# Convolution inside the recurrence before it, and gates as three rounded products, in a two-block kernel

## The chip, the cores and the metric

The kernel runs on one core of one Trainium2 chip. A core has five engines with a queue of instructions each: TensorE (PE in the profile; its weight loads are PEld) multiplies matrices into PSUM, VectorE (DVE) and ScalarE (ACT) work element by element, GpSimd (POOL) too, but it can't reach PSUM, and SyncE (SP) issues the DMAs here. Engines wait for one another through semaphores. The metric is the device time of one execution in microseconds.

## The reference, cut to what matters

Two blocks of two layers each run on a sequence of 512 tokens of width 1024, in float32. The change touches only the first layer of the first block, the even layer:

```
h = rmsnorm(x, norm_pre)
xa, za, xb, gb, gc, zb = split(h @ w_in)                 # 6 x 1024 columns
ua = centred_dwconv(xa, conv_w, left=2) + conv_b         # 4 taps
ya = rg_lru(ua, gates 0, forward) + rg_lru(ua, gates 1, reverse)
ya = ya * silu(za)
yb = gb * centred_dwconv(gc * xb, sc_w, left=1) * silu(zb)   # 3 taps
y = concatenate([ya, yb]) @ w_out
x = x + rmsnorm(y, norm_post)

def rg_lru(u, gate_w, gate_b, lam, reverse):
    r, i = sigmoid(per head of 128: u @ gate_w + gate_b)     # two gates
    log_a = -8 * r * softplus(-lam)
    a = exp(log_a)
    b = sqrt(-expm1(2 * log_a)) * (i * u)
    return scan: h[t] = a[t] * h[t-1] + b[t]
```

There are 8 heads of 128 channels; each has four gate matrices of 128x128 (two gates in each of two directions). The rest, a gated linear attention layer and then a block with feed-forward layers and two kinds of attention, is the same in both kernels.

## The kernel before, in words

Activations lie transposed: 128 channels on the partitions, 512 tokens along the free axis. A large float32 product is made as three products of rounded parts: each operand is split into a high part (rounded to the type fp32r) and a low part (what is left), and the kernel adds high x high, high x low and low x high (`product`, L364 to L366, three matmuls of 128x512 per 128 rows of the sum). GpSimd splits the weights, slot by slot: a slot is 128x1024 weights, a cast (L332) makes the high part and a subtraction (L334) the low one. Raw slots lie in a ring of four, the parts in two buffers each, so GpSimd may split slot s once slot s-2 is used (`slots_used`), and SyncE may load slot s once slot s-4 is split (`w_ready`).

The even layer goes head by head; the code calls a head's 128 channels a channel, numbered 0 to 7, with two copies of its buffers (index `jj`). A channel takes six slots (xa, xb, gc, gb, zb, za), each 24 matmuls into one of four PSUM banks in turn. ScalarE moves each bank to SBUF (`even_moved`, L1325), which frees it for the slot four further on. Below, slot 11 is the last of channel 1, and bank (1,1) is the one of channel 1's second slot.

Per channel the other work is this, in program order. VectorE (`even_dve`): the 4-tap convolution of xa into `ua` (L1778 and three times L1781, signal `ua_ready`), the short 3-tap convolution and its products (L1805 to L1815), then the recurrence: the factors (L1821, L1823, L1825, once per direction), the scans (L1829, L1832) and the sum (L1834, L1836, signal `even_channel_done`). TensorE (`even_gates`, L664): four plain float32 matmuls of the gate weights `gw` with `ua`, behind the six slots of the channel (behind slot 6 for channel 0); the profile shows eight records per channel. ScalarE (`even_act`): the six moves, sigmoids behind the gates (L1337, L1338), exp and tanh (L1346, L1348, signal `decay_ready`), and a square root per direction behind VectorE's factors (L1355). SyncE: for each channel from 2 on, wait for the channel two before to be done, load the gate weights (L594), then the six slots of weights (L591).

Behind channel 7's gates TensorE goes on to the output products (L712 to L714). They need the rounded parts of y: ScalarE makes the high part of each of 16 tiles (L1360), VectorE the low part (L1842), seven tiles of yb first and then seven of ya, behind channel 6. A channel of the profile's timeline is 36.1 us: six slots of 5.44 and the gates.

In the profile's names arena is the region that holds `gw`, `ua`, `xa_pad` and most tiles; ring holds the raw weights and, in the unused end of its slots, a few tiles of the recurrence; w_tails likewise.

## Time and profile before

| | |
|---|---|
| median of 3 runs | 2734.67 us (2733.76 to 2736.94) |
| the profiled execution | 2738.84 us |
| its span in the profile | 2737.1 us |
| TensorE busy | 2702.6 us, 99% |
| VectorE busy | 1324.9 us, 48% |
| GpSimd busy | 1632.3 us, 60% |
| ScalarE busy | 710.4 us, 26% |
| mean granted TensorE clock | 0.999 |

Busy times are of engines that work at the same time, so they don't add up to the span. A matmul record is longer (0.39 us) than its distance to the next (0.23 us), because matmuls are pipelined: TensorE's pace is read from starts. In the timeline a bracket behind a row gives the idle time ahead of it and what ended it.

### The profile page before, as it was taken

The numbers are of one execution on the slowest core, as the hardware profiler recorded it, in microseconds if no ns is written. First come the engines' busy times: TensorE is split into PE (matmuls) and PEld (weight loads), VectorE is DVE, ScalarE is ACT, GpSimd is POOL, SyncE is SP. The second block draws the span as 40 slices with busy tenths as digits, with TensorE's granted clock in tenths as the row PEclk, the third lists the DMA queues.
The fourth block names the chain that finished last, engine by engine and source line by source line (L and its number), as shares of the span: only waits on it lengthen the run. The fifth ranks groups of instructions, "written<-read, shape, count | busy, mean of one in ns | idle before, by whom it ended". The sixth has DMA issues, their size and how long they took to land.

```text
span 2737.1 us, 36086 instructions
## 1 busy us (share of the span) xinstructions
PE 2702.6 (99%) x13190; PEld 2169.5 (79%) x13190; DVE 1324.9 (48%) x1613; ACT 710.4 (26%) x1243; POOL 1632.3 (60%) x949
## 2 busy tenths in 40 slices
PE   9999999999999999999999999999999999999999
PEld 6777778877888888867888888788888776888887
DVE  7888824474532461176440433642244777543242
ACT  4433413343200110184210113410012476211010
POOL 4566755524665666603666666666566789566565
PEclk9999999999999999999999999999999999999999
DMA  4322222202332322201232332333232100233232
GB/s 180 101 92 91 94 93 85 83 26 70 93 116 78 102 96 93 92 9 43 96 107 85 100 100 88 128 100 111 82 98 94 55 2 2 85 100 115 77 97 87
DMA packets 62028, 235.58 MB, mean 86 GB/s; under 512 B 6880, under 2 KB 7008, under 8 KB 61792
## 3 DMA queue, kind: packets, MB, share of 16 engines
q1 hardware_dynamic: 61920, 234.14, 26.6%
q8 instruction: 68, 1.11, 0.2%
q14 instruction: 40, 0.33, 0.0%
HBM read 232.02 MB, written 2.10 MB: 86 GB/s over the span
## 4 chain that ended last, share of the span: by engine, by line
PE 81%; DVE 5%; POOL 4%; PEld 3%; issue 2%; ACT 1%; DVEq 1%; DMA 1%; PEldq 0%; POOLq 0%; ACTq 0%; SPq 0%
PE ps L364 23%; PE ps L365 23%; PE ps L366 23%; POOL arena L2467 4%; PE ps L1045 2%; PE ps L388 1%; PE ps L382 1%; PE ps L383 1%; PE ps L1029 1%; PEld ps L712 1%; PEld ps L713 1%; PEld ps L714 1%; PE ps L1061 1%; DMA ring<-in_even_in 0%; DVE w_tails L1832 0%
## 5 line engine op out<-in xcount | busy, mean ns | idle before, releaser
L334 POOL TENSOR_TENSOR w_lo<-ring,w_hi 128x1024 fp32r<-128x1024 f32 (+2 forms) x382 | 992.3, 2598 | 56.5 <-issue 3.1
L332 POOL CAST w_hi<-ring 128x1024 fp32r<-128x1024 f32 (+2 forms) x382 | 435.9, 1141 | 906.2 <-PE ps L366 720.7
L364 PE MATMUL ps<-hi,w_hi 128*128 128x512 f32 x2064 | 809.9, 392 | 6.1 <-POOL w_lo L334 3.2
L366 PE MATMUL ps<-hi,w_lo 128*128 128x512 f32 x2064 | 804.0, 390 | 0.0
L365 PE MATMUL ps<-lo,w_hi 128*128 128x512 f32 x2064 | 803.8, 389 | 0.0
L364 PEld LDWEIGHTS ps<-hi,w_hi 128*128 128x128 f32 x2064 | 387.8, 188 | 93.6 <-POOL w_lo L334 6.0
L365 PEld LDWEIGHTS ps<-lo,w_hi 128*128 128x128 f32 x2064 | 387.9, 188 | 82.1 <-issue 2.4
L366 PEld LDWEIGHTS ps<-hi,w_lo 128*128 128x128 f32 x2064 | 387.7, 188 | 81.0
L364 PE MATMUL ps<-hid_hi,w_hi 128*128 128x512 f32 x704 | 274.4, 390 | 0.0
L365 PE MATMUL ps<-hid_lo,w_hi 128*128 128x512 f32 x704 | 274.0, 389 | 0.0
L366 PE MATMUL ps<-hid_hi,w_lo 128*128 128x512 f32 x704 | 273.9, 389 | 0.0
L2051 DVE TENSOR_TENSOR hid_lo<-arena,hid_hi 128x512 f32 (+1 forms) x88 | 222.1, 2524 | 80.2 <-ACT hid_hi L1516 80.2
L1514 ACT ACTIVATE ps<-ps 128x512 f32<-128x512 f32 x88 | 51.2, 582 | 629.4 <-DVE ps L2043 629.4
L2067 DVE SCALAR_TENSOR_TENSOR res<-ps,res 128x512 f32<-128x512 f32 x64 | 44.3, 692 | 343.8 <-PE ps L366 343.8
L2048 DVE TENSOR_TENSOR arena<-arena,ps 128x512 f32<-128x512 f32 x88 | 60.5, 688 | 275.4 <-PE ps L366 274.9
L1516 ACT ACTIVATE hid_hi<-arena 128x512 f32 (+1 forms) x88 | 55.7, 633 | 410.8 <-DVE arena L2048 410.8
L364 PEld LDWEIGHTS ps<-hid_hi,w_hi 128*128 128x128 f32 x704 | 132.1, 188 | 28.8 <-POOL w_lo L334 1.3
L366 PEld LDWEIGHTS ps<-hid_hi,w_lo 128*128 128x128 f32 x704 | 132.1, 188 | 27.6
L365 PEld LDWEIGHTS ps<-hid_lo,w_hi 128*128 128x128 f32 x704 | 132.1, 188 | 27.2
L2467 POOL TENSOR_SCALAR arena<-arena 128x512 f32<-128x512 f32 (+3 forms) x124 | 133.2, 1094 | 14.8 <-DVE arena L2343 14.7
L246 DVE SCALAR_TENSOR_TENSOR lo<-res,consts,hi 128x512 fp32r<-128x512 f32 x64 | 117.5, 1845 | 32.0 <-ACT hi L240 31.8
L2043 DVE TENSOR_TENSOR ps<-ps,rinv 128x512 f32<-128x512 f32 x88 | 61.5, 699 | 117.8 <-PE ps L366 107.8
(369 smaller groups left out, 3326.8 us busy)
## 6 DMA issues: line engine op xcount, KB each, us to landing
ring<-in_ffn_in SPq DMA_DIRECT2D x176, 512.0 KB, 3.5
ring<-in_even_in SPq DMA_DIRECT2D x48, 512.0 KB, 4.6
ring<-in_ffn_out SPq DMA_DIRECT2D x32, 768.0 KB, 4.2
ring<-in_ffn_out SPq DMA_DIRECT2D x32, 640.0 KB, 3.8
ring<-in_even_out SPq DMA_DIRECT2D x16, 512.0 KB, 3.5
ring<-in_sb_qk SPq DMA_DIRECT2D x12, 512.0 KB, 3.5
ring<-in_odd_v SPq DMA_DIRECT2D x8, 512.0 KB, 3.5
ring<-in_odd_r SPq DMA_DIRECT2D x8, 512.0 KB, 3.5
```

The source lines that it names most:

```text
L246: nc.vector.scalar_tensor_tensor(lo[:, t, :], res[:, t, :], con("g_" + f)[:, t:t + 1], hi[:, t, :].bitcast(F32), ALU.mult, ALU.subtract).t ...
L332: nc.gpsimd.tensor_copy(high[:, j % 2, 0:cols], ring[:, j, 0:cols])
L334: nc.gpsimd.tensor_tensor(low[:, j % 2, 0:cols], ring[:, j, 0:cols], high[:, j % 2, 0:cols].bitcast(F32), ALU.subtract).then_inc(sem["w_re ...
L364: nc.tensor.matmul(bank, w_hi[:, j % 2, w], x_hi[:, k, :], start=(k == 0), stop=False)
L365: nc.tensor.matmul(bank, w_hi[:, j % 2, w], x_lo[:, k, :], start=False, stop=False)
L366: mm = nc.tensor.matmul(bank, w_lo[:, j % 2, w], x_hi[:, k, :], start=False, stop=(k == kt - 1))
L1045: mm = nc.tensor.matmul(ps[:, bank + e, col:col + T - t2 * P], neg_tri_r[:, :] if t2 == t else neg_ones_r[:, :], part[softplus_of(p, x2)][ ...
L1516: nc.scalar.activation(hid_hi[:, 2 * i + j, :], wide[:, j, :], ACT.Copy)\
L2043: V.tensor_tensor(gate, gate, rinv[:, :], ALU.mult).then_inc(sem["gate_scaled"], 1)
L2048: V.tensor_tensor(wide[:, j, :], wide[:, j, :], up, ALU.mult).then_inc(sem["hidden_wide"], 1)
L2051: V.tensor_tensor(hid_lo[:, 2 * i + j, :], wide[:, j, :], hid_hi[:, 2 * i + j, :].bitcast(F32), ALU.subtract)\
L2467: op = G.tensor_scalar(part, part, coef[:, s % 4, i, e:e + 1], None, ALU.mult)
```

## The change

1. The gates become three products of rounded parts. ScalarE rounds the gate weights of a channel (`gw_hi`, one buffer per `jj`) and its tile (`ua_hi`, one buffer); GpSimd makes the low part of the weights (`gw_lo`) in two halves of 128x256, which it puts between its slots; VectorE makes the low part of the tile (`ua_lo`).
2. VectorE's convolution of channel c+1 moves into the recurrence of channel c, between the factors and the scans, and `ua_lo` of c+1 between the two scans. For this ScalarE moves the first bank of c+1 ahead of the square roots of c; it rounds the tile behind them, ahead of the other five moves.
3. SyncE loads the first four slots of a channel ahead of its gate weights; the wait for a finished channel stands in front of the gate weights and of slots 4 and 5.

```diff
@@ SyncE
                         for jj in range(2):
-                            sp.wait_ge(sem["even_channel_done"], 2 * i + (jj + 3))
-                            gate_weight(i + 1, jj)
                             for n in range(6):
                                 s = 6 * jj + n
+                                if n == RING:
+                                    sp.wait_ge(sem["even_channel_done"], 2 * i + (jj + 3))
+                                    gate_weight(i + 1, jj)
                                 sp.wait_ge(sem["w_ready"], 12 * i + (s + 13))
                                 even_weight(i + 1, s)
@@ TensorE
             def even_gates(i, jj):
-                pe.wait_ge(sem["ua_ready"], 2 * i + (jj + 1))
+                pe.wait_ge(sem["gates_split"], 4 * i + (2 * jj + 2))
                 pe.wait_ge(sem["gates_read"], 2 * i + (jj + 1))
-                pe.wait_ge(gate_landed[jj], 16 * i + 16)
+                pe.wait_ge(sem["ua_low"], 2 * i + (jj + 1))
                 for g in range(4):
-                    mm = nc.tensor.matmul(ps[:, 4 + g, :], gw[:, jj, g * P:(g + 1) * P], ua[:, jj, :],
-                                          start=True, stop=True)
+                    w = slice(g * P, (g + 1) * P)
+                    nc.tensor.matmul(ps[:, 4 + g, :], gw_hi[jj][:, w], ua_hi[:, :], start=True, stop=False)
+                    nc.tensor.matmul(ps[:, 4 + g, :], gw_lo[:, jj, w], ua_hi[:, :], start=False, stop=False)
+                    mm = nc.tensor.matmul(ps[:, 4 + g, :], gw_hi[jj][:, w], ua_lo[:, :], start=False, stop=True)
@@ ScalarE
+            def gates_high_act(i, jj):
+                act.wait_ge(gate_landed[jj], 16 * i + 16)
+                nc.scalar.activation(gw_hi[jj][:, :], gw[:, jj, 0:4 * P], ACT.Copy).then_inc(sem["gates_high"], 1)
+
+            def ua_high_act(i, jj):
+                act.wait_ge(sem["ua_ready"], 2 * i + (jj + 1))
+                nc.scalar.activation(ua_hi[:, :], ua[:, jj, :], ACT.Copy).then_inc(sem["ua_high"], 1)
+
             def even_act(i, jj, c=None):
                 act.wait_ge(sem["even_channel_done"], 2 * i + (jj + 1))
...
+                for n in range(0 if c == 0 else 1, 6):
+                    even_move(i, jj, n, c)
+                    if c == 0 and n == 1:
+                        ua_high_act(0, 0)
...
+                else:
+                    gates_high_act(i + jj, 1 - jj)
                 par = gw[:, jj, 4 * P:4 * P + 16]
                 act.wait_ge(sem["gates_done"], 2 * i + (jj + 1))
+                act.wait_ge(sem["even_channel_done"], 2 * i + (jj + 2))
...
                 a.then_inc(sem["decay_ready"], 1)
+                if c != RG_HEADS - 1:
+                    even_move(i + jj, 1 - jj, 0)
...
                     nc.scalar.activation(rg[d], tg[d], ACT.Sqrt, scale=-1.0).then_inc(sem["root_b_ready"], 1)
+                if c != RG_HEADS - 1:
+                    ua_high_act(i + jj, 1 - jj)
@@ VectorE
+            def convolve(i, jj, c=None):
+                par = gw[:, jj, 4 * P:4 * P + 16]
+                dve.wait_ge(gate_landed[jj], 16 * i + 16)
+                if c != 0:
+                    V.tensor_copy(nsp_c[:, jj, :], nsp2[:, 2 * i + jj, :])
+                dve.wait_ge(sem["even_moved"], 12 * i + (6 * jj + 1 + RING))
+                V.tensor_scalar(ua[:, jj, :], xa_pad[:, jj, 0:T], par[:, 4:5], par[:, 8:9], ALU.mult, ALU.add)
...
+            def ua_lower(i, jj):
+                dve.wait_ge(sem["ua_high"], 2 * i + (jj + 1))
+                V.tensor_tensor(ua_lo[:, :], ua[:, jj, :], ua_hi[:, :].bitcast(F32), ALU.subtract).then_inc(sem["ua_low"], 1)
...
                     V.tensor_tensor(ig[:, d, :], ig[:, d, :], ua[:, jj, :], ALU.mult)
+                if not last:
+                    convolve(i + jj, 1 - jj)
                 for d in range(2):
...
                     V.tensor_tensor_scan(hg[d][:, way], ag[:, d, way], tg[d][:, way], 0.0, ALU.mult, ALU.add)
+                    if d == 0 and not last:
+                        ua_lower(i + jj, 1 - jj)
@@ GpSimd
+            def split_gates(i, jj, half):
+                w = slice(2 * P * half, 2 * P * half + 2 * P)
+                pool.wait_ge(sem["gates_high"], 2 * i + (jj + 1))
+                pool.sem_inc(sem["split_begun"], 1)
+                nc.gpsimd.tensor_tensor(gw_lo[:, jj, w], gw[:, jj, w], gw_hi[jj][:, w].bitcast(F32), ALU.subtract)\
+                    .then_inc(sem["gates_split"], 1)
...
+                for s in range(12):
+                    split_slot(pool, "even_in", 3 * i + (3 + s // RING), s % RING)
+                    if s % 6 in (2, 3):
+                        split_gates(i + 1, s // 6, s % 6 - 2)
```

ScalarE's order behind channel 0, before: tanh, square roots, then the moves of channel 1 (arena<-ps).

```order
L1348 ACTIVATE w_tails<-ring,arena 128x512 x2
L1355 ACT_TABLE_LOAD
L1355 ACTIVATE ring<-w_tails 128x512 [waits factor_ready] x2
L1325 ACTIVATE arena<-ps 128x512 [waits slots_used,even_channel_done]
L1325 ACTIVATE arena<-ps 128x512 [waits slots_used] x3
L1325 ACT_TABLE_LOAD
```

The same place after; gw_hi is rounded between the sixth move and the sigmoids, ua_hi is the rounded tile of channel 1.

```order
L1373 ACTIVATE w_tails<-ring,arena 128x512 x2
L1331 ACTIVATE arena<-ps 128x512 [waits slots_used]
L1382 ACT_TABLE_LOAD
L1382 ACTIVATE ring<-w_tails 128x512 [waits factor_ready] x2
L1339 ACTIVATE ua_hi<-arena 128x512 [waits ua_ready]
L1331 ACTIVATE arena<-ps 128x512 [waits slots_used,even_channel_done]
L1331 ACTIVATE arena<-ps 128x512 [waits slots_used] x2
L1331 ACT_TABLE_LOAD
```

One move went ahead of the square roots; the others now follow a wait for `ua_ready`.

VectorE's order in the recurrence of channel 0, before: factors, scans, sum, then the convolution of channel 1.

```order
L1821 TENSOR_TENSOR w_tails<-arena 128x512
L1823 SCALAR_TENSOR_TENSOR w_tails<-w_tails 128x512
L1825 TENSOR_TENSOR arena<-arena 128x512
L1829 TENSOR_TENSOR w_tails<-arena,ring 128x512 [waits root_b_ready]
L1832 SCALAR_TENSOR_TENSOR w_tails<-arena,w_tails 128x512
L1829 TENSOR_TENSOR w_tails<-arena,ring 128x512 [waits root_b_ready]
L1832 SCALAR_TENSOR_TENSOR w_tails<-arena,w_tails 128x512
L1834 TENSOR_TENSOR w_tails<-w_tails 128x512
L1836 TENSOR_TENSOR arena<-w_tails,arena 128x512
L1773 COPY arena<-arena 128x2 [waits gate_landed_1]
L1778 TENSOR_SCALAR arena<-arena 128x512 [waits even_moved]
```

And after, from the same first instruction on.

```order
L1859 TENSOR_TENSOR w_tails<-arena 128x512
L1861 SCALAR_TENSOR_TENSOR w_tails<-w_tails 128x512
L1863 TENSOR_TENSOR arena<-arena 128x512
L1777 COPY arena<-arena 128x2 [waits gate_landed_1]
L1779 TENSOR_SCALAR arena<-arena 128x512 [waits even_moved]
L1782 SCALAR_TENSOR_TENSOR arena<-arena 128x512 x3
L1869 TENSOR_TENSOR w_tails<-arena,ring 128x512 [waits root_b_ready]
L1872 SCALAR_TENSOR_TENSOR w_tails<-arena,w_tails 128x512
L1788 TENSOR_TENSOR ua_lo<-arena,ua_hi 128x512 [waits ua_high]
L1869 TENSOR_TENSOR w_tails<-arena,ring 128x512 [waits root_b_ready]
L1872 SCALAR_TENSOR_TENSOR w_tails<-arena,w_tails 128x512
```

Five instructions of the convolution and the one of `ua_lo` came into the recurrence.

SyncE's order in the loop, before: the wait for a channel, the gate weights, then the slots.

```order
L594 ISA [waits even_channel_done]
L594 DMA arena<-in_gates 128x528
L619 ISA
L591 ISA [waits w_ready]
L591 DMA ring<-in_even_in 128x1024
```

After, the last of the four slots that are ahead now, the wait, and slot 4.

```order
L597 ISA [waits w_ready]
L597 DMA ring<-in_even_in 128x1024
L624 ISA
L600 ISA [waits even_channel_done]
L600 DMA arena<-in_gates 128x528
L626 REGISTER_ALU
L597 ISA [waits w_ready]
L597 DMA ring<-in_even_in 128x1024
```

The wait for a finished channel went behind four slots of weights.

## Rows read from the trace of the kernel before

**Rows 1.** The page: busy us (share of the span) and instructions.

```profile
PE 2702.6 (99%) x13190; PEld 2169.5 (79%) x13190; DVE 1324.9 (48%) x1613; ACT 710.4 (26%) x1243; POOL 1632.3 (60%) x949
```

**Rows 2.** By stretch: PE, PEld, DVE, ACT, POOL busy us; granted clock, DMA share, GB/s.

```profile
100.00:200.00 100.00, 99.81 (x423) 79.13 (x423) 82.21 (x62) 34.70 (x48) 64.64 (x34) 1.00 0.27 89
...
92.00:95.00 3.00, 3.00 (x9) 2.31 (x8) 0.03 (x1) 2.99 (x5) 2.86 (x2) 0.50 0.54 175
```

**Rows 3.** Timeline, PE and ACT: start us, us, engine, instruction, [idle before <-releaser].

```profile
193.34 0.60 ACT L1325 ACTIVATE arena<-ps 128x512 f32<-128x512 f32 x1 [3.54 <-PE ps L366]
198.78 0.60 ACT L1325 ACTIVATE arena<-ps 128x512 f32<-128x512 f32 x1 [4.84 <-PE ps L366]
...
198.58 3.59 PE L664 MATMUL ps<-arena 128*128 128x512 f32 x8
202.24 0.39 PE L365 MATMUL ps<-lo,w_hi 128*128 128x512 f32 x1
```

**Rows 4.** Timeline of PE: waits, and matmuls behind them.

```profile
13.30 0.65 PE L654 MATMUL ps<-y_lo,w_hi 128*128 128x512 f32 x1 [1.81 <-DVE y_lo L1735]
...
74.20 0.50 PE L364 MATMUL ps<-hi,w_hi 128*128 128x512 f32 x1 [1.28 <-ACT arena L1325]
...
91.53 0.50 PE L364 MATMUL ps<-hi,w_hi 128*128 128x512 f32 x1 [2.71 <-POOL w_lo L334]
...
95.51 0.40 PE L365 MATMUL ps<-lo,w_hi 128*128 128x512 f32 x1
...
165.80 0.50 PE L364 MATMUL ps<-hi,w_hi 128*128 128x512 f32 x1 [0.19 <-POOL w_lo L334]
...
274.73 0.50 PE L364 MATMUL ps<-hi,w_hi 128*128 128x512 f32 x1 [0.33 <-POOL w_lo L334]
...
312.39 0.51 PE L712 MATMUL ps<-lo,w_hi 128*128 128x512 f32 x1 [0.59 <-DVE y_lo L1842]
...
586.29 1.10 PE L849 MATMUL ps<-consts,arena 128*128 128x128 f32 x8 [1.52 <-ACT arena L1473]
```

**Rows 5.** Timeline of SP's queue and POOL; last, the gate weights' time to landing.

```profile
82.19 0.35 SPq L594 DMA_DIRECT2D arena<-in_gates  x1
...
87.53 1.20 POOL L332 CAST w_hi<-ring 128x1024 fp32r<-128x1024 f32 x1 [10.23 <-DMA ring<-in_even_in]
...
DMA to landing us min/median/max: 2.7/2.8/8.3
```

**Rows 6.** Timeline of PE and DVE, gates 0 to the convolution of channel 1.

```profile
52.97 3.59 PE L664 MATMUL ps<-arena 128*128 128x512 f32 x8
...
59.36 0.69 DVE L1805 TENSOR_TENSOR arena<-arena 128x512 f32<-128x512 f32 x1
...
72.92 0.68 DVE L1825 TENSOR_TENSOR arena<-arena 128x512 f32<-128x512 f32 x1
...
81.90 0.16 DVE L1773 COPY arena<-arena 128x2 f32<-128x2 f32 x1
...
82.60 2.41 DVE L1781 SCALAR_TENSOR_TENSOR arena<-arena 128x512 f32<-128x512 f32 x3
```

**Rows 7.** Timeline of POOL and DVE, a factor of channel 4's recurrence.

```profile
209.02 2.66 POOL L334 TENSOR_TENSOR w_lo<-ring,w_hi 128x1024 fp32r<-128x1024 f32 x1
...
209.50 2.72 DVE L1823 SCALAR_TENSOR_TENSOR w_tails<-w_tails 128x512 f32<-128x512 f32 x1
```

**Rows 8.** Timeline of ACT and DVE: first sigmoid, first factor, end of the recurrence.

```profile
199.39 1.28 ACT L1337 ACT_TABLE_LOAD   x1
202.21 0.69 ACT L1337 ACTIVATE ring<-ps,arena 128x512 f32<-128x512 f32 x1 [1.54 <-PE ps L664]
...
208.60 0.82 DVE L1821 TENSOR_TENSOR w_tails<-arena 128x512 f32<-128x512 f32 x1 [5.33 <-ACT w_tails L1348]
...
228.65 0.16 DVE L1773 COPY arena<-arena 128x2 f32 x1
```

**Rows 9.** Timeline of PE and DVE at the end of the layer.

```profile
307.51 3.59 PE L664 MATMUL ps<-arena 128*128 128x512 f32 x8
...
308.86 6.49 DVE L1842 TENSOR_TENSOR y_lo<-arena,lo 128x512 fp32r<-128x512 f32 x7 [1.57 <-ACT lo L1360]
```

**Rows 10.** Groups of POOL's instructions by shape: busy us, mean ns.

```profile
L2461 POOL TENSOR_TENSOR arena<-arena 128x248 f32<-128x248 f32 x8 | 4.8, 604 | 0.0
```

## What I predict, and how it follows

> **What bounds the kernel now.** I read the page first: TensorE is busy 2702.6 us, 99% of the span [rows 1], so only TensorE's own work and its few waits can move the time. The change touches the even layer alone, the first 310 us, so I went on to the busy times by stretch: in its steady part VectorE is busy 82 of 100 us [rows 2]. The reader should see there that the engine that feeds TensorE has little to spare. Next come TensorE's gate products in the timeline [rows 3] and every idle stretch before a matmul of this layer [rows 4]. There are two kinds: a wait for ScalarE to empty a bank (74.20) and waits for GpSimd's split weights (91.53, 165.80, 274.73). The rows of the DMA queue say where the second kind comes from: in the loop the queue waits for a whole channel to be done, issues the gate weights at 82.19 and only then the next projection slots, so GpSimd idles 10.23 us for them [rows 5].
>
> **The gate products.** A channel's four gates begin at 198.58 and the second matmul behind them at 202.24. A slot of 24 matmuls takes 5.44 us (two bank moves stand 5.44 apart), 0.227 each, so four gates cost 202.24 - 198.58 - 0.23 = 3.43 us [rows 3]. Twelve matmuls of rounded parts, of the same 128x512 shape, cost 12 x 0.227 = 2.72. Saved: 8 x 0.71 = **5.7 us**, all on TensorE's path. The bound above is nothing saved, if the new operands ran at another pace; the existing products of rounded parts say they don't.
>
> **The waits that go.** The projection DMAs of a channel's first four slots no longer wait for a channel to be done. So the waits at 91.53 (2.71), 165.80 (0.19) and 274.73 (0.33) go. The first also cost clock: the ten matmuls from 91.53 to 95.51 took 3.98 us where 2.27 is their pace, so 1.7 more: from 92 to 95 the granted clock is 0.50 [rows 2], the 1.2 GHz level. The same slow start shows behind the 1.81 wait at 13.30, and the 1.52 at 586.29 is the longest that I found without it [rows 4]. The wait at 74.20 (1.28) goes too, since the move of the next channel's first bank now stands ahead of the square roots. With 0.1 of slow start behind each: 4.4 + 0.3 + 0.4 + 1.4 = **6.5 us**.
>
> **The new wait in channel 1.** The moves of banks 1 to 5 of the next channel now stand behind the rounding of its convolved tile, and this behind the convolution, which stands behind VectorE's six factor instructions. TensorE needs bank (1,1) empty to begin slot 11. Gates 0 begin at 52.97 [rows 6], end at 55.69, and four slots later it is 77.45. VectorE: the low part of the first tile (0.7) puts the chain behind it 0.7 later, so the short convolution begins at 60.1 and not 59.36. From there to the end of the sixth factor instruction before took 73.60 - 59.36 = 14.2 us, so 74.3. The convolution with its first instructions is 3.1 us (81.90 to 85.01, [rows 6]). If only its last instruction meets GpSimd, the tile is ready at 78.0; adding 0.60 for the rounding and 0.60 for the move, as a bank move's row, bank 1 is free at 79.2, a wait of 1.8. The other end: VectorE instructions with two operands in SBUF wait for a running GpSimd instruction (started 0.48 behind a subtraction of 2.66, a factor took 2.72 and ended 0.54 behind it, [rows 7], where a free one of its kind takes about 0.7, as 72.92 in [rows 6]). TensorE runs 0.7 ahead of before here, so GpSimd's subtraction of slot 11 starts at 73.9, before the last factor instruction; that one ends at 76.9, and two of the three long convolution instructions stand behind the cast and the subtraction of slot 12 (77.7 to 81.6). The tile is ready at 82.4, the bank free at 83.6: a wait of 6.2. I take 6.2, since the 0.7 shifts work that way on both engines. With 1.7 of clock behind it: **+7.9** (bounds +1.8 and +7.9).
>
> Before, the convolution of channel 1 ran unhindered (three instructions in 2.41 at 82.60, [rows 6]), in the gap in which GpSimd idled until 87.53 for its DMA [rows 5]. Now the gap is closed and the convolution stands among the splits.
>
> The Trainium skill ("SBUF — State Buffer", section "Who interferes with whom") says that the two engines share a port pair as an exclusive lock, and that the one that issues second is blocked until the first has ended. The rows agree (ended 0.54 behind the other's end). It speaks against the place to which the convolution moves; if the two engines only shared bandwidth there, this term would be near its lower end and the total some 6 us lower.
>
> **The two added splits per channel on GpSimd.** A 128x248 GpSimd subtraction takes 0.60 [rows 10], so about 0.65 each. They stand behind slots 2 and 3, where GpSimd idles: cast and subtraction take about 3.9 of a slot's 5.44 us (the subtraction 2.66, [rows 7], the cast 1.2, [rows 5]). Nothing on the path; without that cover 0.65 each, at most 1.3 a channel. The queue's wait for a channel to be done now holds up the weights of slots 4 and 5 only; they land some 5 us behind it and are wanted 20 us later, so nothing.
>
> In ScalarE's order of the two kernels the reader sees the rounding of the tile come between the square roots and the moves, in VectorE's the convolution between the factors and the scans, and in the queue's the wait go behind four weights.
>
> **The loop of the recurrence.** The gate weights of channel c+2 are now fetched behind channel c, and ScalarE rounds them before the sigmoids of c+1. Done(c) to landing is 0.2 + 2.8 [rows 5], rounding 0.6, table load 1.3, sigmoids to the first factor 208.60 - 202.21 = 6.4 [rows 8]: 11.3. The recurrence took 228.65 - 208.60 = 20.05, and now holds the convolution (3.1) and the low part (0.7) as well: 35.1 with no more lock waits, 36.8 with one of 1.7 more. TensorE's period becomes 6 x 5.44 + 2.72 = 35.37. Where the loop is longer, VectorE falls behind by up to 1.4 a channel, and the slack at bank 1 (about 4 us in the steady state) is gone after three. I put **+1.0** on it, one such wait (bounds 0 and +6.8, five of them).
>
> **The output products.** They need the low parts of y, the first of them behind channel 6. Before, the first stood at 308.86, 1.35 behind the start of gates 7 (307.51), and TensorE waited 0.59 for the third [rows 4, 9]. After, gates 6 begin at 77.45 + 6.2 + 5.44 + 1.7 (gates 1) and 5 x 35.37 later, 267.6. Channel 5 is done about there, the recurrence of 6 starts 11.3 to 12 later and takes 20.05 + 3.8, and up to 2 more of lock: channel 6 is done between 303 and 305.8. The first low part is 0.7 more if free, 2.7 if it meets GpSimd: 304 to 308.5. TensorE wants it 38.1 behind gates 6, at 305.7. I take 2.5 us of wait, since locks have decided every such place so far; it is over the 1.81 that cost clock: 2.5 + 1.7 - 0.7 = **+3.5** (bounds 0 and +3.8).
>
> **Sum**: -5.7 - 6.5 + 7.9 + 1.0 + 3.5 = +0.2 us. The profiled execution took 2738.84, so 2739.0; against the median of the three runs, 2734.67, this is 2734.9.
>
> **Rivals.**
> 1. *The convolution slips through (faster).* The wait at slot 11 is at its lower end, under the 1.81 that cost clock: -5.7 - 6.5 + 1.8 + 0 + 3.5 = -6.9, with the end wait at its lower bound -10.4. For it: the lock waits are a matter of tenths. Against it: VectorE is shifted late and GpSimd early. About 2726. Chance 0.22.
> 2. *The loop is longer than TensorE's period (slower).* With 36.8 against 35.37 TensorE waits 1.4 for bank 1 in each of channels 3 to 7: -5.7 - 6.5 + 7.9 + 6.8 + 3.5 = +6.0, so 2740.7. It decides from a loop of about 36.2. For it: VectorE's 82%, and the closed gap. Against: a lock wait may fall on idle time. Chance 0.15.
> 3. *The clock does not fall in the new waits*: -3.4, 2731.5. It is inside the range of the forecast. Chance 0.10.
> My forecast, gain and new waits cancelling: 0.53.
>
> **Range and chances.** 0.2% is 5.5 us, about what a measurement of this kernel tells from no change. Faster by more: rival 1, 0.22. Slower by more: rival 2, 0.15. Within: 0.63. The range, 2726 to 2741, holds the forecast and most of both; the forecast's own is 2731 to 2738.
>
> **What would show it.** Right: twelve matmuls at 0.227 per channel in 2.7 us; no TensorE wait on the split weights behind gates 1; one wait of 2 to 6 us before slot 11 for ScalarE's move, some 21.8 us behind gates 0, and slow matmuls behind it; VectorE instructions of 2.7 us in the convolution; a wait of about 2.5 us on VectorE at the first output product. Wrong: no wait at slot 11 (then 2726 or less), or one in most channels (2740).

## The result, and the profile after

The changed kernel takes 2745.53 us (median of 7 runs, 2744.01 to 2746.0), the kernel before 2734.67 (7 runs, 2733.76 to 2738.95). The ratio is 1.0032 with a 95% interval of 1.0023 to 1.0042: slower by 0.3%. I had forecast 2734.9 and a range up to 2741; the time lies outside.

The two profiled executions stand 6.8 us apart (2738.84 and 2745.67), the medians 10.9. The one of before lay high among its own runs, which scatter from 2733.7 to 2739.3 in all that follows (their median was 2736.2 to 2736.8 in samples of 21 to 33). The traces place the loss that they hold: the first matmul of line 382, the next layer's, starts at 408.67 us before and 415.07 after, 6.4 later, and what follows it takes 2328.4 and 2328.8. So I compare kernels by that start as well. It names the place; the medians say how much. Where in the kernel before its runs differ is open, since only one of them was traced.

The page of after, first part (busy us, share of the span, instructions), answers to [rows 1]:

```profile
PE 2697.5 (98%) x13222; PEld 2175.6 (79%) x13222; DVE 1315.6 (48%) x1621; ACT 718.6 (26%) x1259; POOL 1647.8 (60%) x965
```

TensorE is busy 5.1 us less than before, and the kernel is slower. So the time went into waits. The waits of PE up to 420 us say into which (total us, times, longest):

```profile
PE ps L364 <- ACT arena L1331: 13.7, 6, 7.1
PE ps L721 <- DVE y_lo L1884: 2.7, 1, 2.7
```

Six waits for ScalarE to empty a bank, and one for the low part of y. The timeline of PE shows them one by one, and the gates of a channel between two of them; it answers to [rows 3, 4]:

```profile
84.99 0.79 PE L364 MATMUL ps<-hi,w_hi 128*128 128x512 f32 x1 [7.14 <-ACT arena L1331]
...
88.57 0.41 PE L366 MATMUL ps<-hi,w_lo 128*128 128x512 f32 x1
...
158.40 0.49 PE L364 MATMUL ps<-hi,w_hi 128*128 128x512 f32 x1 [0.66 <-ACT arena L1331]
...
195.59 0.49 PE L364 MATMUL ps<-hi,w_hi 128*128 128x512 f32 x1 [1.47 <-ACT arena L1331]
...
201.16 0.39 PE L672 MATMUL ps<-ua_hi,gw_hi 128*128 128x512 f32 x1
...
203.88 0.39 PE L364 MATMUL ps<-hi,w_hi 128*128 128x512 f32 x1
...
232.71 0.49 PE L364 MATMUL ps<-hi,w_hi 128*128 128x512 f32 x1 [1.47 <-ACT arena L1331]
269.88 0.49 PE L364 MATMUL ps<-hi,w_hi 128*128 128x512 f32 x1 [1.46 <-ACT arena L1331]
307.09 0.49 PE L364 MATMUL ps<-hi,w_hi 128*128 128x512 f32 x1 [1.55 <-ACT arena L1331]
318.29 0.47 PE L721 MATMUL ps<-lo,w_hi 128*128 128x512 f32 x1 [2.70 <-DVE y_lo L1884]
```

The twelve products of rounded parts take 203.88 - 201.16 = 2.72 us. The wait at slot 11 is 7.14, and the first eight matmuls behind it take 3.58 where eight take 1.82, so 1.76 more, the usual 0.1 of slow start included. Then there is a wait in each of the channels 3 to 7, and 232.71 - 195.59 = 37.12 is the period, where TensorE's own work is 35.37.

The slot-11 wait, read from VectorE, GpSimd and ScalarE (timeline of each):

```profile
74.64 2.88 DVE L1863 TENSOR_TENSOR arena<-arena 128x512 f32<-128x512 f32 x1
77.45 0.69 DVE L1777 COPY arena<-arena 128x2 f32<-128x2 f32 x1
78.05 1.32 DVE L1779 TENSOR_SCALAR arena<-arena 128x512 f32<-128x512 f32 x1
79.46 4.33 DVE L1782 SCALAR_TENSOR_TENSOR arena<-arena 128x512 f32<-128x512 f32 x3
```

```profile
74.31 2.65 POOL L334 TENSOR_TENSOR w_lo<-ring,w_hi 128x1024 fp32r<-128x1024 f32 x1
76.94 1.18 POOL L2446 TENSOR_TENSOR gw_lo<-arena,gw_hi 128x256 fp32r<-128x256 f32 x1
78.06 1.04 POOL L332 CAST w_hi<-ring 128x1024 fp32r<-128x1024 f32 x1
79.24 2.34 POOL L334 TENSOR_TENSOR w_lo<-ring,w_hi 128x1024 fp32r<-128x1024 f32 x1
```

```profile
83.82 0.63 ACT L1339 ACTIVATE ua_hi<-arena 128x512 fp32r<-128x512 f32 x1 [8.44 <-DVE arena L1782]
```

The last factor instruction and the convolution stand among four GpSimd instructions that follow each other almost without a gap (0.14 us at most), and take 9.2 us where such instructions took 3.8 before (0.68 and 3.1, [rows 6]). The copy ends at 78.14, 0.02 behind the gate split that ran beside it. Such time, in which a VectorE instruction is held up by a running GpSimd instruction, is called a lock wait below; the profile counts it as busy time of VectorE. The tile is ready at 83.8 and the bank free at 85.

The loop of a steady channel (DMA queue, ScalarE, VectorE):

```profile
206.35 0.33 SPq L600 DMA_DIRECT2D arena<-in_gates  x1
```

```profile
209.13 0.64 ACT L1335 ACTIVATE gw_hi<-arena 128x512 fp32r<-128x512 f32 x1 [7.17 <-DMA arena<-in_gates]
```

```profile
203.51 2.63 DVE L1878 TENSOR_TENSOR arena<-w_tails,arena 128x512 f32 x1 [0.17 <-issue]
...
217.46 1.77 DVE L1859 TENSOR_TENSOR w_tails<-arena 128x512 f32<-128x512 f32 x1 [6.21 <-ACT w_tails L1373]
...
226.44 4.99 DVE L1782 SCALAR_TENSOR_TENSOR arena<-arena 128x512 f32<-128x512 f32 x3
...
240.63 2.63 DVE L1878 TENSOR_TENSOR arena<-w_tails,arena 128x512 f32 x1 [0.17 <-issue]
```

A channel is done at 206.14 (203.51 + 2.63). Then the gate weights are fetched, ScalarE has waited 7.17 us for them, rounds them, loads its table, does the sigmoids and the exp and tanh, and the first factor starts at 217.46: 11.3 us. The recurrence ends at 243.26, 25.8 later. 11.3 + 25.8 = 37.1, TensorE's new period. The ring closes on itself: done, gate weights, rounding, sigmoids, recurrence, done.

### The profile page after: what moved, and what is told of

Same layout as the page of the kernel before. It is cut to its first block, busy times and chain, and to the rows that moved or that the text cites. A ratio compares the mean times of both kernels' runs of the same rounds, so it can differ in the third digit from the quotient of the medians.

```text
span 2743.9 us, 36206 instructions
## 1 busy us (share of the span) xinstructions
PE 2697.5 (98%) x13222; PEld 2175.6 (79%) x13222; DVE 1315.6 (48%) x1621; ACT 718.6 (26%) x1259; POOL 1647.8 (60%) x965
## 4 chain that ended last, share of the span: by engine, by line
PE 76%; DVE 8%; POOL 4%; PEld 3%; DVEq 2%; ACT 2%; issue 2%; DMA 1%; PEldq 0%; ACTq 0%; POOLq 0%; SPq 0%
PE ps L364 21%; PE ps L366 21%; PE ps L365 21%; POOL arena L2522 4%; PE ps L1054 2%; PE ps L388 1%; PE ps L382 1%; PE ps L383 1%; DVE arena L1782 1%; PE ps L1038 1%; PEld ps L721 1%; PEld ps L722 1%; PEld ps L723 1%; DVE w_tails L1861 1%; DVEq L1867 1%
## 5 line engine op out<-in xcount | busy, mean ns | idle before, releaser
L364 PE MATMUL ps<-hi,w_hi 128*128 128x512 f32 x2064 | 808.7, 392 | 16.0 <-ACT arena L1331 13.7
L365 PE MATMUL ps<-lo,w_hi 128*128 128x512 f32 x2064 | 803.9, 389 | 0.0
L364 PEld LDWEIGHTS ps<-hi,w_hi 128*128 128x128 f32 x2064 | 387.8, 188 | 101.9 <-issue 10.5
L365 PEld LDWEIGHTS ps<-lo,w_hi 128*128 128x128 f32 x2064 | 387.9, 188 | 81.5 <-issue 1.4
L364 PE MATMUL ps<-hid_hi,w_hi 128*128 128x512 f32 x704 | 274.4, 390 | 0.0
L365 PE MATMUL ps<-hid_lo,w_hi 128*128 128x512 f32 x704 | 273.9, 389 | 0.0
L364 PEld LDWEIGHTS ps<-hid_hi,w_hi 128*128 128x128 f32 x704 | 132.1, 188 | 28.8 <-POOL w_lo L334 1.3
L365 PEld LDWEIGHTS ps<-hid_lo,w_hi 128*128 128x128 f32 x704 | 132.1, 188 | 27.4
L246 DVE SCALAR_TENSOR_TENSOR lo<-res,consts,hi 128x512 fp32r<-128x512 f32 x64 | 100.9, 1585 | 31.9 <-ACT hi L240 31.7
```

What stands on the lines that cost most here:

```text
L246: nc.vector.scalar_tensor_tensor(lo[:, t, :], res[:, t, :], con("g_" + f)[:, t:t + 1], hi[:, t, :].bitcast(F32), ALU.mult, ALU.subtract).t ...
L364: nc.tensor.matmul(bank, w_hi[:, j % 2, w], x_hi[:, k, :], start=(k == 0), stop=False)
L365: nc.tensor.matmul(bank, w_hi[:, j % 2, w], x_lo[:, k, :], start=False, stop=False)
```

## Experiments

Theory T: two causes. The slot-11 wait comes from VectorE's chain (factors, convolution) meeting GpSimd's splits; the waits of the later channels come from the loop "channel done, gate weights fetched and rounded, sigmoids, recurrence", which at 37.1 is longer than TensorE's 35.4. Rivals stand with each experiment. Each kernel was timed beside the kernel before on one chip; the experiments used two chips, so kernels are compared by their ratios to it, given with 95% intervals. The last column is the time from the layer's first matmul of line 364 (at about 25 us) to the first of line 382. The start alone also holds what happened ahead of the change's work: 24.75 us before, 24.99 in the changed kernel, 23.34 with late rounding and early decay terms together, 26.10 with bank 1 first.

| kernel | median us (range, runs) | ratio | start of L382 | L364 to L382 |
|---|---|---|---|---|
| before | 2734.67 (2733.76 to 2738.95, 7) | | 408.67 | 383.92 |
| changed | 2745.53 (2744.01 to 2746.0, 7) | 1.0032 (1.0023 to 1.0042) | 415.07 | 390.08 |
| new queue order alone | 2740.96 (2738.46 to 2742.35, 11) | 1.0013 (1.0004 to 1.0022) | 411.05 | 386.17 |
| rounded gates alone | 2740.99 (2740.4 to 2744.98, 11) | 1.0019 (1.001 to 1.0028) | 412.92 | 388.06 |
| convolution and queue, plain gates | 2731.44 (2729.82 to 2731.84, 11) | 0.9981 (0.9972 to 0.999) | 401.77 | 376.93 |
| the same, decay terms early | 2732.16 (2730.4 to 2732.58, 11) | 0.9985 (0.9976 to 0.9994) | 402.63 | 377.60 |
| changed, old queue | 2757.75 (2756.39 to 2759.35, 5) | 1.0079 (1.0066 to 1.0093) | 427.3 | 402.30 |
| changed, late rounding | 2739.41 (2737.76 to 2740.54, 11) | 1.001 (1.0001 to 1.0019) | 410.09 | 384.61 |
| changed, bank 1 first | 2743.66 (2740.41 to 2746.54, 11) | 1.0025 (1.0016 to 1.0035) | 412.78 | 386.68 |
| changed, decay early | 2741.8 (2740.12 to 2743.02, 11) | 1.0018 (1.0009 to 1.0027) | 412.01 | 387.03 |
| changed, late rounding, decay early | 2733.59 (2731.57 to 2734.57, 11) | 0.9989 (0.998 to 0.9998) | 402.19 | 378.85 |
| changed, all three moves | 2734.9 (2733.48 to 2737.43, 11) | 0.9996 (0.9987 to 1.0005) | 404.25 | 379.27 |
| changed, short subtraction | 2726.74 (2725.31 to 2727.11, 5) | 0.9963 (0.9949 to 0.9977) | 396.94 | 371.70 (L365 to L383 there) |

**Gate weights rounded behind tanh.** ScalarE no longer waits for their DMA ahead of the sigmoids.

```diff
-                else:
-                    gates_high_act(i + jj, 1 - jj)
...
                 if c != RG_HEADS - 1:
                     even_move(i + jj, 1 - jj, 0)
+                    gates_high_act(i + jj, 1 - jj)
```

> The changed kernel, with ScalarE's rounding of the next channel's gate weights moved from ahead of the sigmoids to behind the tanh. Theory (the loop): in the changed kernel ScalarE waits 7.17 us for the gate weights' DMA ahead of each steady channel's sigmoids, which makes the loop from one finished channel to the next 37.1 us against TensorE's 35.4. With the rounding out of the loop the five waits of 0.66 to 1.55 us for bank 1 go and 6.6 us with them; the 7.1 us wait at slot 11 stays, a wait of 2 to 3 at the first output product too: about 2739. Rival (VectorE alone is too slow, through its lock waits with GpSimd): the waits stay, 2745.

2739.41, and the traces differ by 5.0 up to line 382 (5.5 from 25 us on). PE's waits, then VectorE's first factor and the end of its recurrence:

```profile
85.47 0.79 PE L364 MATMUL ps<-hi,w_hi 128*128 128x512 f32 x1 [7.13 <-ACT arena L1331]
230.11 0.49 PE L364 MATMUL ps<-hi,w_hi 128*128 128x512 f32 x1 [0.40 <-ACT arena L1331]
```

```profile
211.35 1.50 DVE L1858 TENSOR_TENSOR w_tails<-arena 128x512 f32<-128x512 f32 x1 [1.31 <-ACT w_tails L1371]
...
238.04 2.64 DVE L1877 TENSOR_TENSOR arena<-w_tails,arena 128x512 f32 x1 [0.17 <-issue]
```

The 6.6 us of the later channels fell to 0.8 (0.40 at 230.11 and again at 302.02) and the slot-11 wait stayed: two causes, and the second is the loop. But the loop got less short than the edit says. The channel before was done at 204.94, so the first factor follows 6.4 us behind it instead of 11.3, 4.9 less; the recurrence takes 240.68 - 211.35 = 29.3 instead of 25.8, 3.5 more, since it now meets more of GpSimd's splits. The period is 35.7, just above TensorE's 35.37.

**Bank 1 of the next channel moved ahead of the rounding of its tile.**

```diff
-                for n in range(0 if c == 0 else 1, 6):
+                for n in range(0 if c == 0 else 2, 6):
...
                 if c != RG_HEADS - 1:
+                    even_move(i + jj, 1 - jj, 1)
                     ua_high_act(i + jj, 1 - jj)
```

> The changed kernel, with the move of the next channel's second bank ahead of the rounding of its tile. Theory (VectorE's chain sets the pace, ScalarE's order only says where TensorE notices it): the waits at slot 5 of each channel go, but TensorE then waits for the low part of the tile ahead of gates 1 (some 5 us), later channels eat up the slack, and the output products wait more; in all 1 to 5 us less than the changed kernel, 2741 to 2744. Rival (ScalarE's order alone is the cause): all 13.7 us of waits and 1.6 of slow clock go, 2731.

2743.66, in the expected range. The wait for the bank became one for the low part of the tile, one slot later. PE, then VectorE:

```profile
90.41 0.77 PE L672 MATMUL ps<-ua_hi,gw_hi 128*128 128x512 f32 x1 [6.00 <-DVE ua_lo L1789]
```

```profile
80.58 4.38 DVE L1783 SCALAR_TENSOR_TENSOR arena<-arena 128x512 f32<-128x512 f32 x3
...
89.60 0.66 DVE L1789 TENSOR_TENSOR ua_lo<-arena,ua_hi 128x512 fp32r<-128x512 f32 x1
```

ScalarE's order alone is not the cause. TensorE wants the gates at 90.41 - 6.00 = 84.41. The tile is ready at 84.96, only 0.55 later, and rounded 0.7 behind that; its low part ends at 90.26, because a product (1.35) and a scan (3.21, where a free one takes 1.23) stand ahead of it in VectorE's order. So most of this wait is the place of the low part. A kernel with the low part right behind the rounding was not run.

**Decay terms ahead of the reciprocal of the norm** (17 small VectorE instructions, 6.8 us in the changed kernel, that stood ahead of channel 0's short convolution).

```diff
-            rinv_dve(dve, "even_pre")
             nsp2 = nsp.rearrange("p (c d) -> p c d", d=2)
+            dve.drain()
+            decay_terms((11, 9, 7, 5, 3, 1))
...
+            V.tensor_copy(nsp_c[:, 0, :], nsp2[:, 0, :]).then_inc(sem["nsp_ready"], 1)
+            rinv_dve(dve, "even_pre")
...
                     scale_plain(5)
-                    decay_terms((11, 9, 7, 5, 3, 1))
```

> The changed kernel, with VectorE's small decay terms moved from channel 0 into its idle 7 us ahead of the first rinv. Theory: VectorE's chain in channel 0 begins 6 to 7 us earlier, so the wait at slot 11 shrinks from 7.1 to about 1 and its slow clock (1.6) goes; the loop of 37.1 per channel stays, with waits of 1.5 at slot 5: about 7 us less, 2738. Rival (the slot-11 wait is made of lock waits that come back wherever the chain starts): under 2 us less, 2744.

2741.8, between the 2738 of the theory and the 2744 of the rival: half of what I had expected. PE's timeline:

```profile
80.50 0.50 PE L364 MATMUL ps<-hi,w_hi 128*128 128x512 f32 x1 [2.02 <-ACT arena L1331]
117.69 0.49 PE L364 MATMUL ps<-hi,w_hi 128*128 128x512 f32 x1 [1.48 <-ACT arena L1331]
...
314.70 0.77 PE L721 MATMUL ps<-lo,w_hi 128*128 128x512 f32 x1 [2.70 <-DVE y_lo L1885]
```

The slot-11 wait fell from 7.14 to 2.02 with no slow clock behind it, but the waits of the loop begin at channel 2 instead of 3 and are 1.48 from the start. In the changed kernel the long wait had given VectorE a lead that the loop then used up. So the two causes share one account: what the first gives back, the second takes, as long as the loop is longer than TensorE's period.

**The new queue order alone, in the kernel before.**

```diff
-                            sp.wait_ge(sem["even_channel_done"], 2 * i + (jj + 3))
-                            gate_weight(i + 1, jj)
                             for n in range(6):
                                 s = 6 * jj + n
+                                if n == RING:
+                                    sp.wait_ge(sem["even_channel_done"], 2 * i + (jj + 3))
+                                    gate_weight(i + 1, jj)
```

> The kernel before, with only the new order of SyncE's queue (four slots of weights ahead of the wait for a finished channel). Theory: the waits for split weights at 91.53 (2.71 and 1.7 of clock), 165.80 and 274.73 go, but GpSimd then splits where it idled, so the convolution of channel 1 runs into locks and gates 1 wait for it: between -4 and +2 us against before, 2731 to 2737. Rival (the queue part is a plain gain): -5.1, 2729.6.

2740.96: this edit only lets DMAs go earlier and makes the kernel slower by 4 us. Both my theory's range (2731 to 2737) and the rival's gain of 5 missed; what I had named, locks in the convolution and gates waiting for it, is there, but larger. PE, VectorE, and PE's window from 90 to 92 us (us, busy and instructions, granted clock, DMA share, GB/s):

```profile
90.20 6.61 PE L665 MATMUL ps<-arena 128*128 128x512 f32 x8 [4.86 <-DVE arena L1782]
96.25 0.80 PE L364 MATMUL ps<-hi,w_hi 128*128 128x512 f32 x1
```

```profile
85.21 4.94 DVE L1782 SCALAR_TENSOR_TENSOR arena<-arena 128x512 f32<-128x512 f32 x3
```

```profile
90.00:92.00 2.00, 1.80 (x2) 0.50 0.53 121
```

The 2.71 us wait for weights is gone, and GpSimd is no longer idle. The convolution of channel 1, which had run in 2.41 in that gap [rows 6], now takes 4.94, and the gates wait 4.86 for it and then run at 1.2 GHz. They take 96.25 - 90.20 - 0.23 = 5.8 us instead of 3.43. Waits and clock together: 1.14 + 4.86 + 2.4 = 8.4, against 6.2 before (1.28 + 2.71 + 1.7 + 0.19 + 0.33), 2.2 more; the traces say 2.3 from 25 us on.

**Rounded gates alone**, convolution and queue as before (`ua_hi` is rounded behind the fifth move).

```diff
-                for n in range(0 if c == 0 else 1, 6):
+                for n in range(6):
                     even_move(i, jj, n, c)
-                    if c == 0 and n == 1:
-                        ua_high_act(0, 0)
+                    if n == (1 if c == 0 else 4):
+                        ua_high_act(i, jj)
...
+                else:
+                    convolve(i, jj, c)
+                    ua_lower(i, jj)
```

> The kernel before with only the gates as three products of rounded parts; convolution and queue as before, ScalarE rounds the tile behind its fifth move, VectorE makes the low part right behind the convolution. Theory: 0.71 us per channel are gained on TensorE, but the queue's wait for a finished channel already has GpSimd just in time (0.19 and 0.33 us late), so TensorE waits for split weights by about what it gained and by the 0.7 us of the low part: 2735 to 2741. Rival (the products are a gain of their own): 2731.

2740.99. PE's timeline:

```profile
77.96 0.80 PE L364 MATMUL ps<-hi,w_hi 128*128 128x512 f32 x1 [5.69 <-ACT arena L1330]
...
204.39 0.50 PE L364 MATMUL ps<-hi,w_hi 128*128 128x512 f32 x1 [0.92 <-POOL w_lo L334]
241.05 0.51 PE L364 MATMUL ps<-hi,w_hi 128*128 128x512 f32 x1 [0.95 <-POOL w_lo L334]
```

The wait at 77.96 comes from the locks too: the move stands behind the square roots, and the last factor that they need ended at 76.8. The 5.7 us that TensorE saves are paid back in the other channels as well: 36.66 from wait to wait, where before it was 36.1. The recurrence takes 21.3 us there, and 20.1 before, and the queue had no room for it (waits of 0.19 and 0.33 before).

**Convolution and queue, with plain float32 gates.**

```diff
                 for g in range(4):
-                    w = slice(g * P, (g + 1) * P)
-                    nc.tensor.matmul(ps[:, 4 + g, :], gw_hi[jj][:, w], ua_hi[:, :], start=True, stop=False)
-                    nc.tensor.matmul(ps[:, 4 + g, :], gw_lo[:, jj, w], ua_hi[:, :], start=False, stop=False)
-                    mm = nc.tensor.matmul(ps[:, 4 + g, :], gw_hi[jj][:, w], ua_lo[:, :], start=False, stop=True)
+                    mm = nc.tensor.matmul(ps[:, 4 + g, :], gw[:, jj, g * P:(g + 1) * P], ua[:, jj, :],
+                                          start=True, stop=True)
```

(the roundings and splits of gate weights and tile are taken out with it)

> The changed kernel with the gates as plain float32 products again, so without the roundings on ScalarE, the low part of the tile on VectorE and the gate splits on GpSimd: the moved convolution and the queue's new order alone. Theory: ScalarE's moves no longer stand behind the convolution and the gate weights' landing is off ScalarE's path, so the waits for bank 1 go; gates 1 wait about 1 to 3 us for the convolved tile; 2731 to 2736. Rival (the convolution inside the recurrence costs time by itself, since it delays the scans): steady waits of over 1 us per channel stay, 2743 or more.

2731.44: faster than both kernels, by 0.19% against before. From 25 to 330 us PE has two waits left; the expected one of gates 1 isn't there. One is this, the other (0.78) is for split weights at 316.73, as before:

```profile
305.46 0.50 PE L719 MATMUL ps<-lo,w_hi 128*128 128x512 f32 x1 [0.72 <-DVE y_lo L1872]
```

So two parts of the change are worth having together, and the third, which saves 5.7 us on the engine that is 99% busy, turns the gain into a loss. In the loop, its rounding ahead of the sigmoids and its low part in the recurrence lengthen the ring, while it shortens TensorE's period to below it: with plain gates a first factor follows a finished channel by 6.4 us where TensorE is not waited for (channels 1 to 2), and the recurrence takes 25.0, so the ring could go round in 31.4, and TensorE's period is 36.1. At slot 11, no bank move stands behind a rounded tile any more. The convolution in the recurrence alone, with plain gates and the old queue, was not run.

**Late rounding and early decay terms together.**

> The changed kernel with both edits that helped alone: gate weights rounded behind the tanh, and VectorE's decay terms ahead of rinv. Theory: the wait at slot 11 is 2 us (as with the early decay terms alone), the steady waits go (as with the late rounding alone), a wait of 2 to 3 at the first output product stays: 5.0 + 3.1 us under the changed kernel plus up to 2 more, since the early start is no longer lost in the loop: 2734 to 2737. Rival (the two gains are the same one): 2739.

2733.59, a little under the expected 2734 to 2737 and 11.9 less than the changed kernel. The traces say 12.9 less up to line 382, but 1.65 of it lies ahead of 25 us, where this execution lost no clock behind a wait of 1.82 at 13.48 us. From 25 us on it is 11.2, and alone the two moves gave 5.5 and 3.1: once the loop is short the early terms give 5.8. The slot-11 wait is 1.46; the output wait:

```profile
304.70 0.47 PE L721 MATMUL ps<-lo,w_hi 128*128 128x512 f32 x1 [2.77 <-DVE y_lo L1884]
```

**All three moves.**

> The changed kernel with all three moves: rounding of the gate weights behind tanh, bank 1 of the next channel ahead of the rounding of its tile, decay terms early. Without the bank's move it took 2733.59, with waits of 1.46 (slot 11), 0.89, 0.40 and 0.40 for banks and 2.77 at the output. Theory: the wait for bank 1 goes, a wait for the low part of the tile ahead of the gates comes in its place and is some 1.1 shorter (as in the kernel with the bank's move alone); the 2.77 at the output stays. 2731 to 2733. Rival (the move of the bank only delays the tile, and the sum stays): 2733.5 to 2735.

2734.9: the rival's figure. The bank waits went, but 0.83 and 1.17 for split weights and a longer output wait (3.49) came; the clock is 0.66 from 306 to 311 us, as it is in the kernel with two moves. Moving one more thing forward no longer helped; from 25 us on the two traces differ by only 0.4.

**Plain gates with early decay terms.**

> The kernel with plain float32 gates, the convolution in the recurrence and the new queue order took 2731.44 us. Here the decay terms move ahead of the reciprocal of the norm as well. Theory (the end of VectorE's recurrence decides only where TensorE waits for it): the kernel with plain gates has no wait for a bank in the whole layer, only 0.5 to 0.8 at places that don't depend on the decay terms, so this gives at most 1 us: 2730.5 to 2731.5. Rival (the decay terms are themselves on the path to the first slots): the 2 to 4 us that the same edit gave to the kernels with rounded gates come again: 2727.5 to 2729.5.

2732.16, and a start of line 382 of 402.63 against 401.77: no gain, and if anything a little slower. Where TensorE had no wait but the 0.7 at the output that VectorE decides, an earlier VectorE was worth nothing. This also speaks against the rival that the decay terms are a cost of their own.

**The changed kernel with the old queue order.**

> The changed kernel with the old order of the queue: the wait for a finished channel stands ahead of all six slots. Theory (the new queue order is what makes room for the longer recurrence): before, TensorE's wait for the split weights of a channel's first slot was 0.2 to 0.3, so nothing was left; the recurrence now holds the convolution and the low part (3.8 us and locks) and ends later, and each of channels 2 to 7 waits 3 to 5 us for split weights: 2755 to 2770. Rival (the queue's order is worth only its waits in the kernel before, and GpSimd's idle time takes the locks away from the convolution, as it did before): 2740 to 2750.

2757.75, as the theory said. PE, VectorE (channel 1's convolution) and GpSimd behind it:

```profile
82.30 0.79 PE L364 MATMUL ps<-hi,w_hi 128*128 128x512 f32 x1 [4.43 <-ACT arena L1330]
95.98 0.51 PE L364 MATMUL ps<-hi,w_hi 128*128 128x512 f32 x1 [2.79 <-POOL w_lo L334]
...
291.35 0.80 PE L364 MATMUL ps<-hi,w_hi 128*128 128x512 f32 x1 [5.33 <-POOL w_lo L334]
```

```profile
78.68 2.42 DVE L1781 SCALAR_TENSOR_TENSOR arena<-arena 128x512 f32<-128x512 f32 x3
```

```profile
92.16 1.28 POOL L332 CAST w_hi<-ring 128x1024 fp32r<-128x1024 f32 x1 [14.04 <-DMA ring<-in_even_in]
```

Here the rival was right in one thing: with GpSimd idle the convolution ran free (2.42 instead of 4.33) and the slot-11 wait is 2.7 shorter. But then five of the six channels 2 to 7 wait for their weights (2.79, 2.33, 2.29, 4.02 and 5.33). The new queue order harms alone and is worth 12 us together with the convolution in the recurrence and the rounded gates: an idle stretch of one engine was the free time of another.

**GpSimd's subtraction cut short.**

```diff
-            nc.gpsimd.tensor_tensor(low[:, j % 2, 0:cols], ring[:, j, 0:cols], high[:, j % 2, 0:cols].bitcast(F32),
+            n_low = 128 if name == "even_in" and not (isinstance(i, int) and i == 0) else cols
+            nc.gpsimd.tensor_tensor(low[:, j % 2, 0:n_low], ring[:, j, 0:n_low], high[:, j % 2, 0:n_low].bitcast(F32),
```

> The changed kernel, with GpSimd's subtraction cut to the first 128 of 1024 columns for the even layer's input slots behind the first four (the low parts of the other columns are old values; its numbers are not the reference's). It takes away most of the time that GpSimd keeps VectorE out and nothing else. Theory (lock waits): VectorE's 2.7 us instructions shrink to about 0.7 in the even layer, the waits at slot 11, in the steady channels and at the first output product all go: some 17 to 20 us under the changed kernel, 2727. Rival (the new order of instructions alone is too long): the waits stay within 2 us in sum, 2743.

2726.74, 0.3 from the expected 2727. No wait at slot 11, none in the loop; at the first output product 1.27 us stay, which I had expected to go. VectorE's timeline of a steady channel:

```profile
200.24 0.73 DVE L1860 TENSOR_TENSOR w_tails<-arena 128x512 f32<-128x512 f32 x1 [7.85 <-ACT w_tails L1374]
...
206.54 2.41 DVE L1783 SCALAR_TENSOR_TENSOR arena<-arena 128x512 f32<-128x512 f32 x3
...
216.23 0.69 DVE L1879 TENSOR_TENSOR arena<-w_tails,arena 128x512 f32 x1 [0.17 <-issue]
...
235.65 0.74 DVE L1860 TENSOR_TENSOR w_tails<-arena 128x512 f32<-128x512 f32 x1 [7.91 <-ACT w_tails L1374]
```

The recurrence takes 216.92 - 200.24 = 16.7 us, and in the changed kernel 25.8: 9 us of every steady channel come from VectorE's lock waits behind GpSimd's long subtractions. The two gate splits per channel are still in this kernel, and without the long subtractions they make no wait on TensorE. The period is 35.41, TensorE's own. This agrees with the Trainium skill ("SBUF — State Buffer", section "Who interferes with whom"): the engine that issues second is blocked until the first has ended; the four rows from 74.64 on show that a two-element copy (0.69, where it took 0.16 before, [rows 6]) is blocked too; it ends with GpSimd's instruction, within 0.02.

## Why the prediction was wrong, point by point

| term | predicted | measured in the traces |
|---|---|---|
| gates | -5.7 | -5.7 (2.72 per channel) |
| waits that go | -6.5 | -6.5, all four gone |
| slot 11 | +7.9 | +8.9 (7.14, 1.76 of clock and slow start) |
| loop of the recurrence | +1.0 | +7.1 (0.66 + 1.47 + 1.47 + 1.46 + 1.55, and 0.1 of slow start each) |
| output products | +3.5 | +2.1 (2.70 - 0.59, no clock lost) |
| sum | +0.2 | +5.9 (the starts of line 382: +6.4; 0.24 of it is there already at 25 us, ahead of the change's work) |

- **The step that failed is the loop term**, "I put +1.0 on it, one such wait (bounds 0 and +6.8, five of them)". The mechanism was named, its parts were near (11.3 from done to the first factor, as measured), and its upper end is what came. I took the recurrence as 20.05 + 3.8 and treated a further lock wait as a chance. It took 25.8, 1.95 more. With the short subtraction it took 16.7, so some 9 of the 25.8 are lock waits behind the long subtractions; less the 3.8 that moved in, 16.7 leaves 12.9, so the old 20.05 held some 7 (an estimate from these figures), and 2 came on top. I had counted such a further lock wait once, in one channel. The recurrences of channels 3 to 6 take 25.8, 25.8, 26.0 and 25.8: the same meetings came back in every channel, so one more wait counted once per channel. Why they repeat was not tested; GpSimd's splits follow TensorE, and in this loop TensorE follows VectorE. The experiment with late rounding took 5.8 of the 6.6 us away: 4.9 less from done to the first factor, of which the recurrence took 3.5 back in lock waits.
- **Slot 11**: the choice of 6.2 between 1.8 and 6.2 was right, for the reason given, and was 0.9 too small: the two-element copy and the first convolution instruction were blocked as well. The copy was held by the gate split at 76.94, a GpSimd instruction that the prediction put at nothing on the path, and the split at 218.63 (1.19) held a factor of the steady recurrence 0.4 longer. No kernel without only these splits was run.
- **Waits that go**: right as a sum. What I missed is that GpSimd's idle gap had a use, although I had noted that the convolution ran in it. The kernel with the queue order alone shows the price.
- **Output products**: a wait of 2.70 against 2.5, but I added 1.7 for the clock, from the one row in which 1.81 cost clock. It didn't.
- **Rival 2** (loop longer than TensorE's period, 2740.7) is what happened, with 37.1 where I had 36.8; I gave it 0.15. Rival 1, the convolution slipping through, is what the kernel with short subtractions shows: 2726.74.
- **The base**: I carried the sum from the profiled execution of before, which was 4.2 above the median of the three. Of the 10.6 us between forecast and result 5.7 are the terms above (5.9 - 0.2); 4.2 are where that execution lay in the scatter of the kernel before, which was not in my range; under 1 I can't place. Against the larger samples of before (2736.2 to 2736.8) the change costs about 9 us rather than 10.9.

## What to carry to other kernels

When work is moved into a chain that closes on itself (done, DMA, rounding, activation, recurrence, done), add up the whole ring and compare it with the period of the busiest engine; cutting that engine's work can make the ring the bound, and a lock wait that comes back counts once per round. Time taken out of such a ring can partly return as lock waits (4.9 out, 3.5 back here). Here channel 1's convolution ran at its own speed because GpSimd idled beside it, so ask of every wait that is removed who worked in it. Test parts of a change together as well as alone: here queue order and gates cost 4.1 and 4.6 us alone, the convolution with the queue order gained 5, and the kernel to keep is that one, with plain gates (2731.44).

## What the runs showed of the hardware

The clock did not follow the length of the wait alone. From 25 us to line 382, in the thirteen traces, the granted clock stayed at 2.4 GHz behind every wait of up to 1.76 us, and was at 1.2 GHz behind every one from 3.23 us on (3.23, 3.49, 4.02, 4.43, 4.86, 5.33, 5.69, 6.00, 7.13 and 7.14). In between it went both ways: 1.2 GHz behind 1.90, 2.33, 2.70 (decay terms early, 314.70), 2.71 and 2.77, and 2.4 GHz behind 1.97, 2.02, 2.29, 2.78, 2.79 and the 2.70 of the changed kernel. The wait near 13.5 us, 1.81 or 1.82 in ten of the traces, was followed by 1.2 GHz in nine of them and not in the tenth. PE's windows of the changed kernel, behind the 7.14 and behind the 2.70 (columns as above):

```profile
85.00:87.00 2.00, 2.00 (x5) 0.50 0.00 0
...
318.00:320.00 2.00, 1.71 (x8) 1.00 0.81 238
```

The same behind the 2.77 of the kernel with late rounding and early decay terms:

```profile
306.00:308.00 2.00, 2.00 (x7) 0.50 0.43 170
```

What tells these apart I did not settle. The four plain float32 gate products of a channel took 5.8 us at the low clock, against 3.43.
